# Hybrid encoder block with product-key experts: half of the far block's expert choice and 18 of its gathered products are made in the query stage

## Chip, cores, metric

The kernel runs on one core of a Trainium2 chip. The metric is the device time in microseconds of one execution, from three runs; a profile of one more execution is what the rows below come from. The engines are named as in the profile: PE (TensorE, its weight loads PEld), DVE (VectorE), ACT (ScalarE), POOL (GpSimd), SP (SyncE, which issues most transfers).

## The reference

One encoder block on 512 tokens of width 1024, in float32: a mixer (input projection, two recurrences, a short convolution, output projection, layer norm), then a layer of product-key experts and a last layer norm. The change is in the expert layer:

```python
q = (xt @ w_q).reshape(t, 8, 2, 128)                 # 8 heads, two halves
s1, s2 = q[:, :, 0] @ k1.T, q[:, :, 1] @ k2.T         # 128 keys each
v1, i1 = top_k(s1, 16);  v2, i2 = top_k(s2, 16)
cand_s = v1[..., :, None] + v2[..., None, :]          # 16 x 16 candidates
top_s, pos = top_k(cand_s, 16)
idx = take(i1 * 128 + i2, pos);  g = softmax(top_s)   # 16 of 16384 experts per head
act = gelu(einsum("cd,ced->ce", xb, u_tab[idx]))
y = einsum("ce,ced->cd", g * act, v_tab[idx])
```

So each token has 128 of 16384 experts, each one row of 1024 in a table u and one in a table v.

## The kernel before

The 512 tokens are four blocks of 128. For three of them (DTOK = 384 tokens) the layer is computed densely: for each of 128 blocks of 128 experts, `gelu(u block x tokens)` is multiplied by a gate matrix, which is zero where an expert was not chosen, and then by the v block. For the last, the "far" block (DT = 3), the chosen rows are gathered from HBM: 128 gathers of u rows (each [128 tokens x 1024], 0.5 MB) with one product and sum on DVE each, a gelu, then 128 gathers of v rows with a multiply-add each.

Each dense u block m goes through the same steps. SP loads `u_raw` (four buffers). PE transposes it in two halves (`turn`), ACT copies each half to `ut_hi` (`upper`), `ut_lo` is the difference (`lower`), PE makes 24 matmuls (`product`), ACT makes the gelu into `gel` (two buffers) and SP stores it to HBM (`activations`). ACT's gelu waits until the store that used its buffer has landed.

The program has four stages, and each engine runs its own list of instructions in order:

- The mixer, to about 341 us.
- The query stage: 16 steps n, one for each head and half, and three more u blocks. PE: query matmuls n, `turn(n + 1)`, `product(n)`, scores n. DVE: the 16 best of 128 scores for four token blocks; in odd steps also the 256 candidates and their 16 best. POOL: `lower(n - 1)`, then the lower half of the weight block, `wq_lo(n)`. Here the lower half of a u block is POOL's, and `turn(n + 1)` and `product(n)` wait for `lower(n)`.
- The gates stage: 77 steps s (u blocks 19 to 95). In blocks of four steps DVE turns the positions of one token block into expert numbers and gates (selection: `places`, `match`, `choose`, softmax); first the far block at s = 0, then block ST = 2, whose gates POOL scatters into the gate matrix in HBM one column at a time, then block 0. For blocks 0 and 1 a loop of 21 steps each (at s = 12 and 44) builds one-hot matrices whose products make the gates; each is stored in seven parts after its loop. I call the steps from one loop to the next the gap, and those behind the second loop the closing. `lower` is DVE's from here on. The far block's gathers are spread by `quarter_uses`; POOL starts gather q when product q - 4 is done (RING = 4 tiles).
- The experts stage: 128 steps n. Up to n = 64 (TAIL) every second step makes one of the last 32 u blocks, so a pair of steps is one product and two output steps; then only outputs. `used_by(n)` spreads what is left of the 256 gathered uses.

U_FROM = 72 is the number of gathered products made before the experts stage.

## Time and profile before

| | |
|---|---|
| median of 3 runs | 1733.19 us (1724.51 to 1734.79) |
| profiled execution | 1738.09 us |
| its span, first to last instruction | 1736.3 us |
| PE, DVE, ACT, POOL busy | 1648.8, 1250.3, 640.1, 822.1 us |
| DMA | 397.16 MB, mean 229 GB/s |

The profile's span lies inside the profiled execution's time; the 1.8 us between them are outside the program's instructions. Busy times of PE are modelled ends of pipelined matmuls, so a share near 95% says that PE has work, not that it is at its peak. "Idle before" is the time for which an engine sat idle, and the name behind the arrow is what ended it.

### The profile page before, as it was taken

Reading aid. Unit: us, or ns where it says so; the run is one execution under the profiler, and the core shown is the slowest. Engines: PE = TensorE matmul, PEld = TensorE weight load, DVE = VectorE, ACT = ScalarE, POOL = GpSimd, SP = SyncE. Lnnn points to the kernel's source line nnn. Section 1 sums busy time; section 2 is a strip of 40 time slices with the busy share of each in tenths; the row PEclk is TensorE's granted clock in tenths of the full one; section 3 lists DMA queues with packets and bytes.
Section 4 is the critical chain, followed back from the end, with each engine's and each line's share of the span. In section 5 each row is a group of like instructions: output and inputs, shape, how many; then the busy total and the mean of one; then the engine's idle time right before and its main releaser. Section 6 shows DMA issues by size and latency. Waiting matters only on the chain.

```text
span 1736.3 us, 23321 instructions
## 1 busy us (share of the span) xinstructions
PE 1648.8 (95%) x8522; PEld 1428.2 (82%) x8522; DVE 1250.3 (72%) x2436; ACT 640.1 (37%) x1053; POOL 822.1 (47%) x542
## 2 busy tenths in 40 slices
PE   7998989699999999999998889999999999999996
PEld 5876644499999999999998878888888887888885
DVE  6667842368888887856776368877777787788756
ACT  3568740323334333333333233333333333333331
POOL 4744520284433478877778234545565563222001
PEclk9999999899999999999999989999999999999998
DMA  8436200433324677799777999998999989999772
GB/s 269 145 103 200 85 0 0 136 116 98 106 79 149 177 189 215 212 316 268 208 203 213 364 372 349 332 347 315 326 321 346 324 311 344 341 355 359 234 233 88
DMA packets 242897, 397.16 MB, mean 229 GB/s; under 512 B 33704, under 2 KB 173408, under 8 KB 242784
## 3 DMA queue, kind: packets, MB, share of 16 engines
q1 hardware_dynamic: 182816, 259.17, 44.1%
q0 software_dynamic: 55296, 134.31, 25.0%
q10 hardware_dynamic: 4672, 2.19, 0.4%
q8 instruction: 68, 1.11, 0.3%
q14 instruction: 45, 0.37, 0.1%
HBM read 349.40 MB, written 46.20 MB: 228 GB/s over the span
## 4 chain that ended last, share of the span: by engine, by line
PE 43%; DMA 10%; DVE 8%; POOL 4%; issue 3%; ACT 1%; SPq 0%; POOLq 0%; DVEq 0%; ACTq 0%
PE bank L1544 24%; PE bank L841 13%; DMA activations<-gel 4%; DMA gathered<-in_peer_v,expert_rows 4%; PE bank L829 3%; POOL gate_matrix L209 3%; PE bank L1422 2%; DVE ut_lo L899 1%; POOL gathered L930 1%; DMA gathered<-in_peer_u,expert_rows 1%; DVE sel L1301 1%; DVE v_lo L1624 1%; DVE gather_sum L946 1%; DMA gate_rows_then_feed<-activations 1%; DVE hit L1291 1%
## 5 line engine op out<-in xcount | busy, mean ns | idle before, releaser
L841 PE MATMUL bank<-xhi,ut_hi 128*128 128x384 f32 x1024 | 355.1, 347 | 0.3 <-ACT gel L867 0.3
L841 PE MATMUL bank<-xhi,ut_lo 128*128 128x384 f32 x1024 | 344.7, 337 | 0.0
L841 PE MATMUL bank<-xlo,ut_hi 128*128 128x384 f32 x1024 | 344.3, 336 | 0.0
L930 POOL DMA_INDIRECT gathered<-in_peer_v,expert_rows x128 | 193.6, 1512 | 233.1 <-DVE gather_sum L946 216.1
L209 POOL DMA_INDIRECT gate_matrix<-gate_values,gate_cells x128 | 225.8, 1764 | 72.6 <-issue 36.9
L1544 PE MATMUL bank<-v_hi,w_hi 128*128 128x512 f32 x768 | 242.3, 397 | 11.0 <-DVE w_lo L1641 11.0
L930 POOL DMA_INDIRECT gathered<-in_peer_u,expert_rows x128 | 162.8, 1272 | 173.5 <-DVE gather_product L942 129.8
L1544 PE MATMUL bank<-v_lo,w_hi 128*128 128x512 f32 x768 | 238.8, 392 | 0.0
L1544 PE MATMUL bank<-v_hi,w_lo 128*128 128x512 f32 x768 | 238.7, 392 | 0.0
L899 DVE TENSOR_TENSOR ut_lo<-bank,ut_hi 128x512 fp32r<-128x512 f32 x216 | 141.8, 685 | 110.4 <-ACT ut_hi L858 104.6
L1578 ACT ACTIVATE v_hi<-gate_rows_then_feed 128x1024 fp32r<-128x1024 f32 x128 | 135.7, 1061 | 218.9 <-PE bank L1544 211.9
L1624 DVE TENSOR_TENSOR v_lo<-gate_rows_then_feed,v_hi 128x1024 fp32r<-128x1024 f32 x128 | 156.4, 1222 | 63.8 <-ACT v_hi L1578 63.1
L841 PEld LDWEIGHTS bank<-xhi,ut_hi 128*128 128x128 f32 x1024 | 194.3, 190 | 0.5 <-issue 0.5
L841 PEld LDWEIGHTS bank<-xlo,ut_hi 128*128 128x128 f32 x1024 | 194.2, 190 | 0.0
L841 PEld LDWEIGHTS bank<-xhi,ut_lo 128*128 128x128 f32 x1024 | 193.4, 189 | 0.0
L942 DVE SCALAR_TENSOR_TENSOR gather_product<-gathered,h 128x1024 f32<-128x1024 f32 x128 | 156.1, 1219 | 41.9 <-DMA gathered<-in_peer_u,expert_rows 38.4
L1544 PEld LDWEIGHTS bank<-v_hi,w_hi 128*128 128x128 f32 x768 | 142.7, 190 | 41.8 <-DVE v_lo L1624 12.1
L946 DVE SCALAR_TENSOR_TENSOR gather_sum<-gathered,expert_gates,gather_sum 128x1024 f32<-128x1024 f32 x128 | 160.7, 1279 | 21.6 <-DMA gathered<-in_peer_v,expert_rows 21.6
L1544 PEld LDWEIGHTS bank<-v_lo,w_hi 128*128 128x128 f32 x768 | 145.6, 190 | 30.8
L1544 PEld LDWEIGHTS bank<-v_hi,w_lo 128*128 128x128 f32 x768 | 145.3, 189 | 31.0
L858 ACT ACTIVATE ut_hi<-bank 128x512 fp32r<-128x512 f32 x256 | 145.4, 604 | 61.5 <-PE bank L829 60.8
L829 PE MATMUL bank<-ident,u_raw 128*128 128x128 f32 x1024 | 142.9, 278 | 23.7 <-DVE ut_lo L899 16.7
(183 smaller groups left out, 2499.4 us busy)
## 6 DMA issues: line engine op xcount, KB each, us to landing
u_raw<-in_peer_u SPq DMA_DIRECT2D x128, 512.0 KB
gate_rows_then_feed<-in_peer_v SPq DMA_DIRECT2D x128, 512.0 KB
gate_rows_then_feed<-gate_matrix SPq DMA_DIRECT2D x128, 192.0 KB
activations<-gel SPq DMA_DIRECT2D x96, 192.0 KB
gate_rows_then_feed<-activations SPq DMA_DIRECT2D x96, 192.0 KB
w_in<-in_w_in SPq DMA_DIRECT2D x28, 512.0 KB, 4.2
gate_matrix<-gate_zeros SPq DMA_DIRECT2D x8, 1024.0 KB, 6.9
wq<-in_peer_wq SPq DMA_DIRECT2D x16, 512.0 KB, 4.4
```

The costliest lines, as they stand in the source:

```text
L209: self.nc.gpsimd.indirect_dma_start(out=self.flat, out_offset=bass.IndirectOffsetOnAxis(ap=self.at[:, k:k + 1], axis=0), in_=self.gate[:, ...
L829: ins = self.nc.tensor.transpose(self.bank[b][:, k * P:(k + 1) * P], raw[:, j * P:(j + 1) * P], self.ident[:, :])
L841: ins = self.nc.tensor.matmul(self.bank[b + (r % 2) * spare][:, 0:DTOK], u[r % 2][:, k, :], x[:, k, 0:DTOK], start=(i == 0), stop=(i == 3 ...
L858: ins = self.nc.scalar.activation(self.hi[r % 2][at], turned, ACT.Copy)
L899: self.nc.vector.tensor_tensor(out=self.lo[r % 2][at], in0=self.bank[b].rearrange("p (k e) -> p k e", k=4), in1=self.hi[r % 2][at].bitcast ...
L930: self.nc.gpsimd.indirect_dma_start(out=self.tile[r][:, :], out_offset=None, in_=self.tables[kind], in_offset=bass.IndirectOffsetOnAxis(ap ...
L942: ins = V.scalar_tensor_tensor(out=self.product[:, :], in0=self.tile[r][:, :], scalar=1.0, in1=self.x, op0=ALU.mult, op1=ALU.mult, accum_o ...
L946: ins = V.scalar_tensor_tensor(out=y, in0=self.tile[r][:, :], scalar=self.gate[:, k:k + 1], in1=y, op0=ALU.mult, op1=ALU.add)
L1422: ins = nc.tensor.matmul(bank[4 + u][:, q * KEYS:(q + 1) * KEYS], second[:, u, q, :], first[:, u, q, :], start=True, stop=True)
L1544: ins = mm(bank[2 + 2 * tb + half][:, :], w[r][:, tb * P:(tb + 1) * P], v[r][:, half * HALF_D:(half + 1) * HALF_D], start=begins, stop=ends)
L1578: S.activation(v_hi[r][:, :], v_raw[r][:, :], ACT.Copy).then_inc(v_hi_ready, 1)
L1624: V.tensor_tensor(out=v_lo[r][:, :], in0=v_raw[r][:, :], in1=v_hi[r][:, :].bitcast(F32), op=ALU.subtract).then_inc(v_lo_ready, 1)
```

## The change

Heads 0 to 3 of the far block are chosen in the query stage: DVE does places, match and choose behind its step 7, the second match and choose behind step 8, softmax and the row list behind step 9; ACT makes the exponent in its step 8. POOL starts four gathers in its iteration 10, and then three in each iteration from 12 on; DVE makes three products at the head of each of its steps 11 to 15 and three behind them, 18 in all. In the gates stage the far block's selection has heads 4 to 7 alone, in three steps, and what follows comes one step earlier; outside of the loops half a gathered product is made a step where it was one. 80 products are made before the experts stage where it was 72; there two a step are used up to n = 64, where it was 2.25, so that 48 are left for the steps behind it (it was 40). The dense gelu has four buffers.

```diff
@@ -55,15 +55,19 @@
 
 MADE = 96
 RING = 4
-U_FROM = 72
+U_FROM = 80
+EARLY_HEADS = 4
+EARLY_USES = (0,) * 11 + (3,) * 5 + (3,)
+U_QUERIES = sum(EARLY_USES)
+GELS = 4
 ST = DT - 1
 NT, PARTS = 4, 7
 GROUPS = P // NT
 LOOP_STEPS = 21
-SELECT_AT = {DT: 0, ST: 4, 0: 8, 1: 33}
-LOOP_AT = (12, 44)
+SELECT_AT = {DT: 0, ST: 3, 0: 7, 1: 32}
+LOOP_AT = (11, 43)
 CLOSING_AT = LOOP_AT[1] + LOOP_STEPS
-SCATTER_AT = 8
+SCATTER_AT = 7
...
-        self.gel = sb("gel", [P, 2, DTOK])
+        self.gel = sb("gel", [P, GELS, DTOK])
         self.loaded = [sem(f"u_loaded{i}") for i in range(self.UB)]
         self.turned, self.hi_ready, self.lo_ready = sem("u_transposed"), sem("ut_hi_ready"), sem("ut_lo_ready")
         self.done, self.ready = sem("act_done"), sem("gelu_ready")
-        self.stored = [sem(f"act_stored{i}") for i in range(2)]
+        self.stored = [sem(f"act_stored{i}") for i in range(GELS)]
...
-        eng.dma_start(act_dram[at, :], self.gel[:, r % 2, :]).then_inc(self.stored[r % 2], 16)
+        eng.dma_start(act_dram[at, :], self.gel[:, r % GELS, :]).then_inc(self.stored[r % GELS], 16)
...
-        after(eng, self.stored[r % 2], 16 * stores)
+        after(eng, self.stored[r % GELS], 16 * stores)
...
+class Selection:
...
+    def places(self, link, tb, q, n):
+
+        V, heads = self.nc.vector, slice(q, q + n)
+        V.tensor_tensor(out=self.ex[:, 0:n, :], in0=self.top[:, tb, heads, :],
+                        in1=self.top[:, tb, heads, 0:1].broadcast_to([P, n, TOPK]),
+                        op=ALU.subtract).then_inc(self.less_max, 1)
+        V.tensor_scalar(out=self.place[:, 0, 0:n, :], in0=self.pos[:, tb, heads, :], scalar1=4, scalar2=None,
+                        op0=ALU.logical_shift_right)
+        V.tensor_scalar(out=self.place[:, 1, 0:n, :], in0=self.pos[:, tb, heads, :], scalar1=TOPK - 1, scalar2=None,
+                        op0=ALU.bitwise_and)
+        link(V.tensor_copy(self.keyf[:, 0:n, :, :], self.key[:, tb, heads, :, :]))
+        link(V.tensor_copy(self.placef[:, :, 0:n * TOPK], self.place[:, :, 0:n, :].rearrange("p s q k -> p s (q k)")))
+
+    def match(self, link, side, n):
+
+        V, shape = self.nc.vector, [P, n * TOPK, TOPK]
+        link(V.tensor_tensor(out=self.hit[:, 0:n, :, :].rearrange("p q k j -> p (q k) j"),
+                             in0=self.placef[:, side, 0:n * TOPK].unsqueeze(2).broadcast_to(shape),
+                             in1=self.iotab[:, :].unsqueeze(1).broadcast_to(shape), op=ALU.is_equal))
+
+    def choose(self, link, side, n):
+
+        V, hit = self.nc.vector, self.hit[:, 0:n, :, :]
+        link(V.tensor_tensor(out=hit, in0=hit, in1=self.keyf[:, 0:n, side, :].unsqueeze(2).broadcast_to([P, n, TOPK, TOPK]),
+                             op=ALU.mult))
+        link(V.tensor_reduce(self.sel[:, side, 0:n * TOPK], hit.rearrange("p q k j -> p (q k) j"), AX.X, ALU.add))
...
+    def list_rows(self, link, far, q, n):
+
+        link(self.nc.vector.scalar_tensor_tensor(
+            out=far.rows[:, q * TOPK:(q + n) * TOPK], in0=self.sel[:, 0, 0:n * TOPK], scalar=float(KEYS),
+            in1=self.sel[:, 1, 0:n * TOPK], op0=ALU.mult, op1=ALU.add))
+        self.nc.vector.sem_inc(far.listed, 1)
+
+
+    def exponent(self, eng, count, n):
+        eng.wait_ge(self.less_max, count)
+        self.nc.scalar.activation(self.ex[:, 0:n, :], self.ex[:, 0:n, :], ACT.Exp).then_inc(self.exp_ready, 1)
...
-        if q == 0:
-            eng.wait_ge(self.listed, 1)
+        if q in (0, EARLY_HEADS * TOPK):
+            eng.wait_ge(self.listed, 1 + q // (EARLY_HEADS * TOPK))
...
+        picks = Selection(nc, sem, sb, "early", EARLY_HEADS, iota, top, pos, key)
+        PICK_AT = 2 * EARLY_HEADS - 1
+        used_by = lambda n: sum(EARLY_USES[:n])
+        assert PICK_AT + 4 <= EARLY_USES.index(3) and len(EARLY_USES) == QC + 1
...
-                    acts.gelu_to_store(eng, n, n, n // 2)
+                    if n == PICK_AT + 1:
+                        picks.exponent(eng, 1, EARLY_HEADS)
+                    acts.gelu_to_store(eng, n, n, n // GELS)
...
+                    for q in range(RING) if n == PICK_AT + 3 else range(used_by(n - 1) + RING, used_by(n) + RING):
+                        far.start(eng, q)
                 for m in range(QC - 1, BY_QUERIES + 1):
                     acts.lower(eng, m, m)
+                    if m == QC - 1:
+                        for q in range(used_by(QC - 1) + RING, used_by(QC) + RING):
+                            far.start(eng, q)
...
+                picks.constants(link)
...
+                    for e in range(used_by(n), used_by(n + 1)):
+                        far.use(eng, e)
...
+                    if n == PICK_AT:
+                        picks.places(link, DT, 0, EARLY_HEADS)
+                        picks.match(link, 0, EARLY_HEADS)
+                        picks.choose(link, 0, EARLY_HEADS)
+                    elif n == PICK_AT + 1:
+                        picks.match(link, 1, EARLY_HEADS)
+                        picks.choose(link, 1, EARLY_HEADS)
+                    elif n == PICK_AT + 2:
+                        link(picks.softmax(eng, link, 1, EARLY_HEADS, far.gate[:, 0:EARLY_HEADS * TOPK]))
+                        picks.list_rows(link, far, 0, EARLY_HEADS)
+                for e in range(used_by(QC), used_by(QC + 1)):
+                    far.use(eng, e)
...
-            if at <= s < at + 4:
+            if at <= s < at + (3 if tb == DT else 4):
...
-            return int(SELECT_AT[0] <= s < LOOP_AT[0])
-        return 4
+            return int(SELECT_AT[ST] <= s < LOOP_AT[0])
+        return 2
...
-    used_by = lambda s: min(U_FROM, sum(quarter_uses(e) for e in range(s)) // 4)
+    used_by = lambda s: min(U_FROM, U_QUERIES + sum(quarter_uses(e) for e in range(s)) // 4)
+    started_by = lambda s: min(U_FROM, used_by(s) + RING) if s else U_QUERIES - EARLY_USES[QC] + RING
...
+            def select_far(part):
+
+                q, n = heads_of(DT)
+                if part == 0:
+                    picks.places(link, DT, q, n)
+                    picks.match(link, 0, n)
+                    picks.choose(link, 0, n)
+                elif part == 1:
+                    picks.match(link, 1, n)
+                    picks.choose(link, 1, n)
+                elif part == 2:
+                    link(picks.softmax(eng, link, nth[DT] + 1, n, far.gate[:, q * TOPK:(q + n) * TOPK]))
+                    picks.list_rows(link, far, q, n)
...
-                for q in range(used_by(s) + RING, min(used_by(s + 1) + RING, U_FROM)) if s else range(RING):
+                for q in range(started_by(s), started_by(s + 1)):
...
-    used_by = lambda n: min(2 * SLOTS, U_FROM + 9 * min(n, TAIL) // 4 + max(n - TAIL, 0))
+    used_by = lambda n: min(2 * SLOTS, U_FROM + 2 * min(n, TAIL) + max(n - TAIL, 0))
...
-                if n < 4:
-                    eng.wait_ge(acts.stored[m % 2], 16 * (MADE // 2))
+                if n < 2 * GELS:
+                    eng.wait_ge(acts.stored[m % GELS], 16 * (MADE // GELS))
                 else:
-                    eng.wait_ge(w_made, n - 3)
+                    eng.wait_ge(w_made, n - 2 * GELS + 1)
```

In the closing the number of uses goes from 12 to 4, in the seven steps of the gap behind the selection from 6 to 3; the rate in the loops stays at 1.25 a step, and so does that of the scatters.

## Rows read from the trace of the kernel before

**Rows 1.** The page: chain that ended last, by engine.

```profile
PE 43%; DMA 10%; DVE 8%; POOL 4%; issue 3%; ACT 1%; SPq 0%; POOLq 0%; DVEq 0%; ACTq 0%
```

**Rows 2.** Windows by stage: length, busy time of engines, granted clock, DMA share, GB/s.

```profile
341.50:537.80 196.30, 194.54 (x1096) 178.47 (x1096) 153.83 (x776) 70.87 (x128) 105.58 (x63) 0.99 0.32 102
...
603.20:737.90 134.70, 134.70 (x932) 134.70 (x931) 112.62 (x260) 49.74 (x128) 104.53 (x70) 1.00 0.76 207
737.90:799.70 61.80, 57.72 (x356) 56.44 (x354) 32.91 (x45) 19.87 (x38) 47.97 (x30) 0.97 1.08 325
799.70:941.40 141.70, 137.75 (x933) 136.54 (x931) 108.53 (x252) 49.93 (x128) 111.93 (x73) 0.99 0.76 201
941.40:1015.60 74.20, 64.55 (x383) 62.48 (x381) 30.32 (x50) 18.11 (x37) 26.95 (x22) 0.95 1.05 360
...
1041.10:1186.60 145.50, 145.50 (x750) 128.85 (x749) 119.75 (x188) 51.33 (x78) 71.30 (x50) 1.00 0.95 344
1186.60:1447.90 261.30, 254.01 (x1289) 223.01 (x1288) 208.42 (x238) 87.23 (x132) 150.58 (x87) 0.99 0.91 322
...
1470.90:1710.70 239.80, 238.49 (x1044) 196.95 (x1044) 177.36 (x223) 85.73 (x118) 33.39 (x33) 0.99 0.84 290
```

**Rows 3.** Timeline, ACT, two steps without gate work: start, duration.

```profile
532.73 0.49 ACT L867 ACTIVATE gel<-bank 128x384 f32<-128x384 f32 x1 [2.54 <-PE bank L841]
...
537.80 0.49 ACT L867 ACTIVATE gel<-bank 128x384 f32<-128x384 f32 x1 [2.56 <-PE bank L841]
```

**Rows 4.** Waits in the closing: engine, line, waited for: total us, times, longest.

```profile
ACT gel L867 <- DMA activations<-gel: 32.3, 6, 9.2
...
PEld bank L829 <- DMA u_raw<-in_peer_u: 8.8, 4, 3.0
```

**Rows 5.** POOL groups by form: count, busy us, mean ns, idle before.

```profile
L209 POOL DMA_INDIRECT gate_matrix<-gate_values,gate_cells x128 | 225.8, 1764 | 72.6 <-issue 36.9 <-DMA gate_matrix<-gate_values,gate_cells 20.5 <-DVEq L1319 15.2
L930 POOL DMA_INDIRECT gathered<-in_peer_v,expert_rows x128 | 193.6, 1512 | 233.1 <-DVE gather_sum L946 216.1 <-issue 15.3 <-DVE gather_product L942 1.7
L930 POOL DMA_INDIRECT gathered<-in_peer_u,expert_rows x128 | 162.8, 1272 | 173.5 <-DVE gather_product L942 129.8 <-issue 25.6 <-DVEq L1323 18.0
```

**Rows 6.** Timeline, POOL, beside the selection.

```profile
590.47 3.67 POOL L209 DMA_INDIRECT gate_matrix<-gate_values,gate_cells  x1 [0.30 <-issue]
```

**Rows 7.** Chain (first row) and DVE timeline, a 3-use step of the experts.

```profile
1192.84 10.58 DMA gathered<-in_peer_v,expert_rows
...
1203.45 1.28 DVE L946 SCALAR_TENSOR_TENSOR gather_sum<-gathered,expert_gates,gather_sum 128x1024 f32<-128x1024 f32 x1 [3.92 <-DMA gathered<-in_peer_v,expert_rows]
```

**Rows 8.** Timeline, DVE, steps 11 and 12 of the query stage.

```profile
476.87 0.89 DVE L1179 MAX8 best<-bank 128x8 f32<-128x128 f32 x4 [3.22 <-PE bank L1142]
...
491.28 0.89 DVE L1179 MAX8 best<-bank 128x8 f32<-128x128 f32 x4
...
499.73 0.89 DVE L1179 MAX8 best<-bank 128x8 f32<-128x128 f32 x4 [3.22 <-PE bank L1142]
```

**Rows 9.** Timeline, DVE, a selection; then the page's row of gathered products.

```profile
540.42 2.29 DVE L1291 TENSOR_TENSOR hit<-placef,iotab 128x2048 bf16<-128x2048 bf16 x1
...
543.95 1.22 DVE L1296 TENSOR_TENSOR hit<-hit,keyf 128x2048 bf16<-128x2048 bf16 x1
...
L942 DVE SCALAR_TENSOR_TENSOR gather_product<-gathered,h 128x1024 f32<-128x1024 f32 x128 | 156.1, 1219 | 41.9 <-DMA gathered<-in_peer_u,expert_rows 38.4
```

**Rows 10.** Timeline, POOL, query stage.

```profile
462.10 2.55 POOL L881 TENSOR_TENSOR ut_lo<-gather_sum,ut_hi 128x512 fp32r<-128x512 f32 x2 [6.57 <-ACT gather_sum L861]
464.60 2.41 POOL L1116 TENSOR_TENSOR wq_lo<-wq,wq_hi 128x1024 fp32r<-128x1024 f32 x1
```

**Rows 11.** Timeline, PE, query stage.

```profile
452.92 1.05 PE L1142 MATMUL bank<-keysT,qT 128*128 128x128 f32 x8
...
459.30 1.04 PE L829 MATMUL bank<-ident,u_raw 128*128 128x128 f32 x8
```

**Rows 12.** Windows at the end of the gap (columns as rows 2).

```profile
790.00:795.00 5.00, 2.51 (x11) 2.54 (x12) 3.12 (x5) 3.09 (x6) 4.08 (x4) 0.68 1.10 394
```

More of the change, by code:

```diff
@@ L1303, in softmax @@
[L1303 to L1313 removed]
+            picks.constants(link)
```

124 lines of the change are left out of this document (55 added, 69 removed).

## Prediction

> **What bounds the kernel now.** I read the chain of waits first: PE alone carries 43% of the span, with DMA 10% and DVE 8% behind [rows 1]. So a change pays only where PE waits, and it costs wherever it makes PE wait. The windows by stage show where that is [rows 2]. In the query stage (341.5 to 537.8) PE is busy 194.54 of 196.3 us: nothing can be won there, and PE itself sets the step. In the first loop of the gates stage (603.2 to 737.9) it is busy throughout. The gap between the loops (737.9 to 799.7, DMA share 1.08), the second loop (141.7 us for the same 21 steps) and the closing (941.4 to 1015.6, DMA share 1.05 at 360 GB/s) are where PE loses time. In the experts stage the window 1041.1 to 1186.6 holds 11 pairs of steps, 13.23 us each, PE busy throughout; 1186.6 to 1447.9 holds 19 pairs in 261.3 us, 9.9 us above 19 x 13.23. From 1470.9 on PE is busy 238.49 of 239.8 us. The eight gathers that the change adds there lie beside it, as DVE has 177.36 us of work in the same window; I put them at nothing.
>
> **Time that the change wins.** (1) Closing. A step without gate work takes 5.05 us, gelu to gelu [rows 3]; 12 of them make 60.6, the window has 74.2, so 13.6 us is the most that can be won. The waits there are gelu for its store (32.3 us in 6) and PE for u_raw (8.8 in 4) [rows 4]. The change uses 4 gathered rows in the closing where there were 12: eight times 0.524 MB (128 rows of 4 KB) is 4.2 MB, at 360 GB/s 11.7 us. Four gelu buffers let a store land nearly four steps late instead of two. I take 12, bounds 5 and 13.6. (2) Gap. 61.8 us less 11 x 5.05 and 1.8 or so for a group of gate matmuls leaves 4.4, with DMA as full as in the closing. Three or four gathers fewer and the spare gelu buffers should take nearly all: 4, bounds 1 and 4.4. (3) Second loop. It is 7.0 us longer than the first. POOL has 2.4 scatters of 1.764 us and 1.25 gathers of 1.272 us a step, each with 0.30 us of issue [rows 5, 6]: 4.95 + 1.97 = 6.9 us against a step of 134.7 / 21 = 6.4. It enters the loop late, since in the gap it has two scatters and one gather, 5.7 us, in 5.05; with half a gather it has 4.9. Over seven steps that is 5 us less delay: I take 5 of the 7.0, bounds 0 and 7. (4) Experts. In a 3-use step DVE waits 3.92 us for a gather that was 10.58 us on its way [rows 7]. At two uses a step each of the four tiles has a whole pair of steps, 13.2 us, for a start (1.512 + 0.30, [rows 5, 6]) and those 10.6. It just fits, with less traffic around it. Of 9.9 I take 9, bounds 5 and 9.9. Together 30, bounds 11 and 35.
>
> The half selection that is left in the gates stage I put at nothing: DVE's saved 6 us lie beside PE, whose steps there run at 5.05 or 0.2 above.
>
> **Time that the change costs: the query stage.** Two steps take 22.86 us. DVE's odd step takes 14.4 (476.87 to 491.28), the even one 5.2, and then DVE idles 3.22 [rows 8]. Added: a match over 2048 elements takes 2.29 us, the product of the two 1.22 [rows 9], and the reduce as long as the match. Half of each is about 1.2, 0.65 and 1.2; with 0.9 for the places, step 7 gets 3.9 us and step 8 gets 3.0; softmax and list put 0.9 into step 9. Eighteen products of 1.22 [rows 9] are 22 us. In all DVE gets 30 us.
>
> The order on POOL is what hurts. POOL runs ahead of DVE: its iteration n makes the lower half of u block n-1, then that of weight block n. In the trace the pair at 462.10 and the wq_lo at 464.60 are iteration 12 [rows 10], while DVE is in step 9. The change makes iteration 10 start the first gathers right behind its wq_lo, at 467.0 - 22.86 = 444.2. The first start waits until the rows are listed, which DVE does at the end of its step 9. That step's scores are made from 452.92 on [rows 11] and before the change DVE took them up at 476.87 - 22.86 = 454.0. Now it is 3.7 us late (3.9 + 3.0 added, 3.22 idle) and takes 14.4 + 0.9: it lists at 473.0. POOL then makes four starts, 1.57 each with issue (479.3), and only after them, in iteration 11, the lower half of u block 10, 2.5 more (481.8). What is queued behind this wait is thus the work that PE needs at 459.30, when the query matmuls end [rows 11]: the transposes of block 11 take over its bank, and product 10 reads it. PE goes on some **22 us** late (bounds 18 and 26).
>
> The same knot is tied again. POOL's iteration n also waits for three products at the head of DVE's step n-1. Where that stands behind an odd step (iterations 13 and 15), counted from the scores of the odd step: DVE is free at 14.65, its first product ends at 15.9, three starts one behind the other end at 20.6, the lower half at 23.1. PE wants it at 17.4 (11.42 + 5.6 + 0.4): 5.7 us each, **11.4** (bounds 0 and 16). The tail (three starts, then three products behind step 15) adds **3**. ACT's Exp in step 8 waits for DVE and puts two table loads before a gelu; PE needs that gelu's bank two steps later, so 0, at most 2. Last, after 2.6 us of idle PE the granted clock was 0.68 over 790 to 795 [rows 12], 1.6 us of full-clock work lost. Four stalls: **5** (0 to 7). The query stage costs 22 + 11.4 + 3 + 5 = 41, bounds 30 and 50.
>
> **Sum.** The profiled execution took 1738.1 us (span 1736.3): 1738.1 + 41 - 30 = 1749. It stands 4.9 above the median of the runs, 1733.2, so for the median I forecast 1733.2 + 11 = **1744 us**.
>
> **Rivals.** *A, POOL's wait is mostly hidden.* If POOL came to its wait only when the list is nearly there, what is left is DVE's overflow: 30 us of work in 13 us of idle time (four times 3.22), 17 at the end of the stage. 1733 + 17 - 30 = 1720. For it: DVE idles in every pair of steps. Against it: the program's order, by which PE can't reach the scores that end the wait's chain any sooner. 0.1. *B, the wait moves (slower).* The closing stays bound by DMA. With gelu's wait gone, gate stores of 1.18 MB, u blocks of 0.52 and gelus of 0.20 are still 1.90 MB a step, 5.3 us at 360 GB/s before any gather, and PE waits for u_raw instead. It decides if a u block lands more than three steps after its issue. Then closing and gap win 6 instead of 16 and the second loop nothing: 41 - 15 = 26, 1759. 0.22. *C, starts get longer beside DVE.* One scatter next to DVE's selection took 3.67 us [rows 6] against a mean of 1.764. If a third of the query stage's starts took 2 us more, each knot would hold 1 to 3 us more, some 8 in all: 1752. 0.1.
>
> The Trainium skill (SBUF — State Buffer, section SBUF: two separate sides) says that VectorE's two-port operations and GpSimd share one pair of ports as an exclusive lock, and that the descriptors of a gather wait for it; by that rule C holds. The one long scatter agrees, the mean shows that most starts are not held.
>
> *The forecast* itself has 0.58, and 1733 to 1756 as its own range.
>
> **How the numbers follow.** About 1% (17 us) tells a change of this kernel from none: 1716 and 1750.5. Slower by more: B 0.2, C 0.07, and 0.1 of the forecast's upper end, 0.37. Faster by more: a third of A and the ends of the gains, 0.06. Between: 0.57. The range 1722 to 1762 takes in B, C and the near edge of A.
>
> **What would show it.** Right: in the query stage one PE gap of about 22 us near 460, ended by POOL's ut_lo, two of 5 to 6, and a stage of about 237 us; POOL's first gather waiting some 29 us for DVE; closing steps of 5.1 to 5.4 us with no wait of gelu for its store; 19 pairs of the experts at 13.2 to 13.4. Wrong: a stage only 17 us longer (A), waits for u_raw over 15 us in the closing (B), starts above 2 us in the query stage (C).

## The result and the profile after

The changed kernel takes 1743.81 us (median of 7 runs, 1741.59 to 1747.21), the kernel before 1733.19 in the 7 runs beside them (1724.16 to 1737.39). The ratio is 1.0076, 95% interval 1.0049 to 1.0103: slower by 0.8%, less than the 1% that I took as the bound. The profiled execution took 1745.51 us, its span 1743.7.

First the chain of waits of the kernel after, by engine.

```profile
PE 60%; DVE 3%; DMA 2%; issue 1%; ACT 1%; SPq 0%; POOL 0%; POOLq 0%; DVEq 0%; ACTq 0%
```

Against [rows 1] DMA has gone from 10% to 2% and DVE from 8% to 3%. Nothing of that tells that the kernel got slower. For this the windows by stage are needed, with the columns of [rows 2]: length, busy PE, PEld, DVE, ACT, POOL, granted clock, DMA share, GB/s.

```profile
338.00:574.00 236.00, 200.08 (x1105) 181.41 (x1103) 186.53 (x824) 76.30 (x134) 129.84 (x82) 0.93 0.39 127
574.00:643.70 69.70, 65.90 (x402) 64.81 (x403) 59.40 (x91) 27.64 (x48) 23.73 (x17) 0.95 0.55 163
643.70:778.20 134.50, 134.50 (x928) 134.47 (x926) 110.54 (x250) 52.12 (x129) 105.46 (x70) 1.00 0.78 207
778.20:838.50 60.30, 56.85 (x362) 55.57 (x360) 30.27 (x46) 17.74 (x37) 46.80 (x31) 1.00 1.09 316
838.50:971.60 133.10, 133.10 (x918) 133.07 (x916) 106.86 (x246) 49.25 (x126) 104.88 (x70) 1.00 0.78 207
971.60:1039.10 67.50, 63.09 (x387) 61.45 (x386) 20.01 (x32) 18.56 (x36) 11.49 (x10) 0.97 1.05 344
1064.50:1210.10 145.60, 145.60 (x751) 128.96 (x750) 115.07 (x175) 51.21 (x78) 67.64 (x45) 1.00 0.90 314
1210.10:1461.10 251.00, 251.00 (x1290) 222.30 (x1289) 195.35 (x227) 87.84 (x132) 141.46 (x78) 1.00 0.92 319
1478.00:1718.00 240.00, 240.00 (x1060) 198.46 (x1058) 188.01 (x233) 87.10 (x119) 42.38 (x42) 1.00 0.89 313
```

Line by line against [rows 2]: the query stage 236.0 (196.3 before), the gap 60.3 (61.8), the second loop 133.1 (141.7), the closing 67.5 (74.2), the 19 pairs of the experts 251.0 (261.3), with PE busy throughout. The windows of gap and second loop are cut one step off the loop, which now comes a step earlier; by the same blocks the second loop is 134.7 against 141.6 (table below). 251.0 / 19 is 13.21 us a pair, which is the 13.23 of the undisturbed pairs. So each of the four places named in the prediction got shorter, and the query stage paid for more than all of them.

Where it paid, PE's timeline shows. The first row is PE's last matmul before it stops, the others are the four that it starts late on.

```profile
456.00 0.39 PE L1241 MATMUL bank<-xhi,wq_lo 128*128 128x512 f32 x1
477.05 2.25 PE L833 MATMUL bank<-ident,u_raw 128*128 128x128 f32 x8 [20.67 <-POOL ut_lo L885]
...
518.33 2.25 PE L833 MATMUL bank<-ident,u_raw 128*128 128x128 f32 x8 [4.93 <-POOL ut_lo L885]
...
548.85 2.25 PE L833 MATMUL bank<-ident,u_raw 128*128 128x128 f32 x8 [5.78 <-POOL ut_lo L885]
...
557.81 0.63 PE L833 MATMUL bank<-ident,u_raw 128*128 128x128 f32 x4 [1.00 <-POOL ut_lo L885]
```

Each time PE waits for `ut_lo`, POOL's lower half. POOL's own timeline says what it was doing instead.

```profile
438.66 2.42 POOL L1198 TENSOR_TENSOR wq_lo<-wq,wq_hi 128x1024 fp32r<-128x1024 f32 x1
470.67 1.20 POOL L1005 DMA_INDIRECT gathered<-in_peer_u,expert_rows  x1 [29.59 <-DVEq L970]
472.17 0.95 POOL L1005 DMA_INDIRECT gathered<-in_peer_u,expert_rows  x1 [0.30 <-issue]
473.43 0.94 POOL L1005 DMA_INDIRECT gathered<-in_peer_u,expert_rows  x1 [0.30 <-issue]
474.68 0.93 POOL L1005 DMA_INDIRECT gathered<-in_peer_u,expert_rows  x1 [0.30 <-issue]
475.63 2.50 POOL L885 TENSOR_TENSOR ut_lo<-gather_sum,ut_hi 128x512 fp32r<-128x512 f32 x2
```

POOL stood 29.59 us at the first gather, until DVE had listed the rows (released from line 970). Then it made four starts in 4.9 us, and only then the lower half for which PE waited.

The reader should also see what this does to DVE, whose load matters below: after the list it has nothing to do, since PE is late with the scores.

```profile
470.08 0.22 DVE L967 SCALAR_TENSOR_TENSOR expert_rows<-sel_early 128x64 int32<-128x64 f32 x1
485.09 0.89 DVE L1267 MAX8 best<-bank 128x8 f32<-128x128 f32 x4 [14.78 <-PE bank L1229]
```

Before, that idle time was 3.22 us [rows 8].

Last the waits in the closing of the kernel after.

```profile
PEld bank L833 <- DMA u_raw<-in_peer_u: 5.8, 5, 2.4
ACT ut_hi L862 <- PE bank L833: 4.9, 3, 2.3
PE bank L833 <- DMA u_raw<-in_peer_u: 4.4, 3, 2.1
```

The 32.3 us of gelu's wait for its store [rows 4] are gone from the list; the waits for `u_raw` are not.

### A table of stages

For all kernels of this study I took the starts of ACT's gelu instructions from the timeline; the dense u blocks are numbered by them, so that the lengths can be compared. "Query" is from the gelu of block 0 to that of block 20; "gates" all from there to block 95 (selection, first loop, gap, second loop, closing); "pairs" the 19 pairs of the experts; "rest" what follows to the end. One profiled execution each.

| kernel | query | first loop | gap | second loop | closing | gates | pairs | rest |
|---|---|---|---|---|---|---|---|---|
| before | 199.3 | 134.7 | 61.9 | 141.6 | 74.2 (12 steps) | 466.0 | 261.3 | 288.3 |
| after | 243.1 | 134.7 | 59.9 | 134.7 | 72.1 (13 steps) | 448.8 | 251.0 | 282.6 |

In the difference of the spans, 7.4 us, stand +43.8 (query), -17.2 (gates), -10.3 (pairs), -5.7 (rest), and -3.1 in the mixer, which the change doesn't touch. The gelu of block 0 starts at 350.2 us in this execution of the kernel before and between 346.3 and 348.2 in the twelve others, so these 3.1 us look like chance in one execution.

### The profile page after: what moved, and what is told of

Same layout as the page of the kernel before. It is cut to its first block, busy times and chain, and to the rows that moved or that the text cites. A ratio compares the mean times of both kernels' runs of the same rounds, so it can differ in the third digit from the quotient of the medians.

```text
span 1743.7 us, 23338 instructions
## 1 busy us (share of the span) xinstructions
PE 1644.4 (94%) x8522; PEld 1427.4 (82%) x8522; DVE 1259.2 (72%) x2452; ACT 644.1 (37%) x1056; POOL 820.4 (47%) x542
## 3 DMA queue, kind: packets, MB, share of 16 engines
q10 hardware_dynamic: 4672, 2.19, 0.4%
## 4 chain that ended last, share of the span: by engine, by line
PE 60%; DVE 3%; DMA 2%; issue 1%; ACT 1%; SPq 0%; POOL 0%; POOLq 0%; DVEq 0%; ACTq 0%
PE bank L1619 29%; PE bank L845 22%; PE bank L833 5%; PE bank L1497 3%; DMA u_raw<-in_peer_u 2%; DVE sel_late L954 1%; DVE ut_lo L903 1%; DVE hit_late L952 0%; DVE hit_late L945 0%; SPq L817 0%; ACT L975 0%; ACT v_hi L1653 0%; POOL rs L1692 0%; DVE bn L1753 0%; DVE h L1795 0%
## 5 line engine op out<-in xcount | busy, mean ns | idle before, releaser
L1005 POOL DMA_INDIRECT gathered<-in_peer_u,expert_rows x128 | 161.0, 1257 | 257.2 <-DVE gather_product L1017 201.1
L213 POOL DMA_INDIRECT gate_matrix<-gate_values,gate_cells x128 | 222.1, 1735 | 56.8 <-issue 36.9
L833 PEld LDWEIGHTS bank<-ident,u_raw 128*128 128x128 f32 x1024 | 121.6, 143 | 66.0 <-issue 42.1
```

The lines of the kernel that those rows point to most:

```text
L213: self.nc.gpsimd.indirect_dma_start(out=self.flat, out_offset=bass.IndirectOffsetOnAxis(ap=self.at[:, k:k + 1], axis=0), in_=self.gate[:, ...
L833: ins = self.nc.tensor.transpose(self.bank[b][:, k * P:(k + 1) * P], raw[:, j * P:(j + 1) * P], self.ident[:, :])
L1005: self.nc.gpsimd.indirect_dma_start(out=self.tile[r][:, :], out_offset=None, in_=self.tables[kind], in_offset=bass.IndirectOffsetOnAxis(ap ...
```

## Experiments

Each ratio is against runs of the kernel before on the same chip. The first four ran together, so did the next four, and the last three; the kernel before had medians of 1732.53, 1732.29 and 1728.96 us beside them, so kernels of different groups are compared by their ratios or by their stages.

### 1. POOL's gathers two iterations later

```diff
-   for q in range(RING) if n == PICK_AT + 3 else range(used_by(n - 1) + RING, used_by(n) + RING):
+   for q in (range(RING) if n == PICK_AT + 5 else range(used_by(n - 2) + RING, used_by(n - 1) + RING)
+             if n > PICK_AT + 5 else ()):
        far.start(eng, q)
...
-   if m == QC - 1:
-       for q in range(used_by(QC - 1) + RING, used_by(QC) + RING):
+   if m in (QC - 1, QC):
+       for q in range(used_by(m - 1) + RING, used_by(m) + RING):
```

> Kernel after, with POOL starting the same 18 + 4 gathers two iterations later in the query stage; DVE's program is unchanged. Theory (POOL's order is what costs): DVE's list comes 8.7 us after POOL reaches the place instead of 29.6, the lower halves of the u blocks are no longer behind a wait that matters, and what is left is DVE's overflow (30 us of work in some 14 of idle time). Query stage of 236 us becomes some 213 to 216, no PE gap above 3 us in it; total 1743.8 - 20 to 23, 1721 to 1724. Rival (DVE's added work is the cost, POOL's wait only shows it): the stage stays near 236 and the time at 1744. Rival (the starts are slow beside DVE): gathers come late, the stage gets to 225, 1733.

Measured: 1730.73 us, ratio 0.9984 (0.9967 to 1.0001). The query stage is 228.7 us, 14.4 less than after and still 29.4 more than before. POOL's wait for the list and PE's timeline:

```profile
471.02 1.20 POOL L1005 DMA_INDIRECT gathered<-in_peer_u,expert_rows  x1 [6.97 <-DVEq L970]
```

```profile
508.03 2.25 PE L833 MATMUL bank<-ident,u_raw 128*128 128x128 f32 x8 [6.78 <-POOL ut_lo L885]
...
536.92 2.25 PE L833 MATMUL bank<-ident,u_raw 128*128 128x128 f32 x8 [8.68 <-POOL ut_lo L885]
...
545.88 0.63 PE L833 MATMUL bank<-ident,u_raw 128*128 128x128 f32 x4 [1.81 <-POOL ut_lo L885]
```

The list wait shrank from 29.59 to 6.97 us and PE's stop at 456 is gone, as expected. But the later stops grew from 4.93 and 5.78 to 6.78 and 8.68. The theory's number (1721 to 1724) was missed by 7 and its stage (213 to 216) by 13: something that the first stop had covered came up. Two things could be it. One is seen in a row, a product that took 6.04 us instead of 1.22, beside two instructions of POOL:

```profile
475.95 6.04 DVE L1017 SCALAR_TENSOR_TENSOR gather_product<-gathered,h 128x1024 f32<-128x1024 f32 x1
...
476.00 2.55 POOL L885 TENSOR_TENSOR ut_lo<-gather_sum,ut_hi 128x512 fp32r<-128x512 f32 x2
...
478.50 2.40 POOL L1198 TENSOR_TENSOR wq_lo<-wq,wq_hi 128x1024 fp32r<-128x1024 f32 x1
```

The other is DVE's load as such. DVE's timeline parts them. From the head of its step 7, at 427.2 us, to its last product, which ends at 561.4, it has no idle time: 134.2 us, where the kernel before has 105.8 for the same steps, 28.4 less. In experiment 9, with the same products and no gathers, 24.8 of these 28.4 are there. So DVE's load sets the length of this stage. PE's stops for `ut_lo` add nothing of their own, since DVE never ran dry behind them, and some 3.6 us are what DVE and POOL do to each other.

### 2. The kernel after with two gelu buffers

```diff
-GELS = 4
+GELS = 2
```

> Kernel after, with two gelu buffers again. Theory (the buffers carry what was won in gap and closing): gelu waits for its store again, some 15 to 30 us in the gap and closing together, and the time is 5 to 9 us more, 1749 to 1753. Rival (the eight gathers fewer are what won it, the buffers follow): gelu's waits stay under 8 us and the time is within 2 us of 1744.

Measured: 1742.24 us, ratio 1.0065 (1.0042 to 1.0087), beside 1.0076 for the kernel after. The waits in its closing:

```profile
ACT gel L871 <- DMA activations<-gel: 30.0, 7, 5.6
...
PEld bank L833 <- DMA u_raw<-in_peer_u: 5.3, 4, 2.0
```

Gelu waits 30 us for its stores again and the closing is 70.6 us for 13 steps, not longer than the 72.1 with four buffers. So that wait costs nothing, and in this kernel the buffers bring nothing.

### 3. The kernel before with four gelu buffers

```diff
+GELS = 4
...
-        self.gel = sb("gel", [P, 2, DTOK])
+        self.gel = sb("gel", [P, GELS, DTOK])
```

(and every `% 2` and `// 2` of the gelus as in the change)

> Kernel before, with four gelu buffers and nothing else. Theory (half of the closing's loss is gelu waiting for its store): the closing of 74.2 us gets to 68 to 70, the gap wins 1 to 3, second loop and experts stay: 1733.2 - 6 to 9, 1724 to 1727. Rival (the closing is bound by DMA, 26.7 MB at 360 GB/s): PE waits for u_raw instead, the closing stays above 73 us, 1731 to 1734.

Measured: 1730.39 us, ratio 0.998 (0.9955 to 1.0005): no difference that can be told. In its closing (73.3 us, before 74.2) PE waits for `u_raw` instead:

```profile
PEld bank L830 <- DMA u_raw<-in_peer_u: 12.2, 6, 3.7
...
PE bank L830 <- DMA u_raw<-in_peer_u: 10.3, 5, 3.4
```

That was 8.8 us in 4 for PEld before [rows 4]. The wait moved, and the closing stayed bound by DMA. The profiled execution here was one of the short ones, 1721.89 us, 8.5 below the median, so the shorter second loop and pairs that the table below has for it are no gain of the median.

### 4. The kernel before with two gathered uses a step

```diff
-    used_by = lambda n: min(2 * SLOTS, U_FROM + 9 * min(n, TAIL) // 4 + max(n - TAIL, 0))
+    used_by = lambda n: min(2 * SLOTS, U_FROM + 2 * min(n, TAIL) + 17 * max(n - TAIL, 0) // 16)
```

> Kernel before, with 2 instead of 2.25 gathered uses a step up to step 64 of the experts stage and 17 in 16 steps behind it; nothing in the query and gates stages. Theory (the ring of four tiles can't turn 3 uses in a step): the 19 pairs of 261.3 us get to 251.4 and the 6 us at the handover to the pure output steps go too: 1733.2 - 16, 1717. Rival (the traffic is only moved, and the output steps at a DMA share of 0.96 to 0.99 give it back): the output steps of 239.8 us get 5 to 15 us longer, 1722 to 1732. Rival (in the changed kernel it was the smaller total of gathers left, 176 against 184, that helped): less than 8 us won, 1725 or more.

Measured: 1718.84 us, ratio 0.9917 (0.9891 to 0.9942). The 19 pairs take 251.0 us (261.3 before) and the rest 284.3 (288.3). So this one line, which needs no product in the query stage, brings what the change brought in the experts stage, all 10.3 us of the pairs and 4.0 of the rest.

### 5. Both of these edits

The kernel before with the edits of experiments 3 and 4.

> Kernel before with two gathered uses a step up to n = 64 of the experts stage and four gelu buffers. The two edits gave 13.7 us and 2 us (not told from none) each by itself. Theory: they add nothing to one another; four buffers are worth nothing where the closing is bound by DMA, so this is 1717 to 1719 (ratio to before 0.991 to 0.993), query stage 199.3, V window 251.0. Rival: the buffers remove gelu's waits for its store in the closing and give 4 us or more on top, 1713 or less.

Measured: 1717.02 us, ratio 0.9905 (0.9871 to 0.9938). Stages: gates 462.7, pairs 251.0, rest 283.8. It is the base for the next kernels, which have four gelu buffers and two uses a step too.

### 6. The early selection alone

From the kernel after: no gather and no product in the query stage.

```diff
-U_FROM = 80
+U_FROM = 72
-EARLY_USES = (0,) * 11 + (3,) * 5 + (3,)
+EARLY_USES = (0,) * 17
...
-   for q in range(RING) if n == PICK_AT + 3 else range(used_by(n - 1) + RING, used_by(n) + RING):
-       far.start(eng, q)
...
-   started_by = lambda s: min(U_FROM, used_by(s) + RING) if s else U_QUERIES - EARLY_USES[QC] + RING
+   started_by = lambda s: min(U_FROM, used_by(s) + RING) if s else 0
```

(outside of the loops one product a step again; the experts' `used_by` as in experiment 4)

> Kernel after with the early choice of four heads alone in the query stage: no gathers and no products there (72 products in the gates stage as before, two uses a step in the experts up to n = 64, then 17/16). Theory: the selection's 8 us on DVE (3.9 in step 7, 3.0 in step 8, 0.9 in step 9) lie in idle times of 3.22 us each and beside PE, so the query stage is 199.3 plus 0 to 2 and the kernel stands 0 to 2 us from the same kernel without it, 1717 to 1721. Rival: the selection itself already delays DVE so that s_used or the banks stop PE; then a good part of the 43.8 us shows here, 1725 or more.

Measured: 1713.2 us, ratio 0.9884 (0.9851 to 0.9917). The query stage takes 199.4 us: choosing the first four heads there costs nothing. Against experiment 5, run beside it, it is 3.8 us less; the intervals of the two ratios overlap. But it takes up DVE's reserve: from the head of step 7 to the end of the stage's work DVE had 12.9 us of idle time before, and here it has 1.3.

### 7. The early selection and the first four starts

```diff
+   for q in range(RING) if n == PICK_AT + 3 else ():
+       far.start(eng, q)
```

> The last kernel plus the first four starts of gathers in POOL's iteration 10 of the query stage, as in the kernel after; no product there (its first is in the gates stage). So this is the first knot alone. Theory: POOL waits some 29 us for the row list, PE idles 20 to 21 us for ut_lo near 456, 2 to 3 us more go to the clock behind it; the query stage is 220 to 224, the kernel 21 to 24 us above the early selection alone, some 1740 to 1743. Rival: PE's delay is partly given back (no backlog on DVE as there are no products), 10 us or less above it; or the knot costs more than its stall (clock), 28 or more.

Measured: 1736.27 us, ratio 1.0016 (0.9995 to 1.0037), 23.1 us above the kernel of experiment 6. The query stage takes 222.0 us, 22.6 more. PE's row:

```profile
476.85 2.25 PE L833 MATMUL bank<-ident,u_raw 128*128 128x128 f32 x8 [20.66 <-POOL ut_lo L885]
```

That is the stop of the kernel after (20.67 us) to 0.01 us, with four starts and no product anywhere in the stage. Of the 1.9 us beside it nearly all is PE at the lower of its clock levels after the stop: the granted clock was 0.50 until 480.3 us, 3.5 us of work. This is the first knot of the prediction, alone.

### 8. Fewer gathers in the gap and the closing, nothing in the query stage

From experiment 5:

```diff
-U_FROM = 72
+U_FROM = 63
...
-        return 4
+        return 2
...
-17 * max(n - TAIL, 0) // 16
+5 * max(n - TAIL, 0) // 4
```

> The first kernel of this batch with 63 products before the experts stage instead of 72: half a gathered product a step in the gap and the closing as in the kernel after, nothing in the query stage, and 5/4 uses a step from n = 64 of the experts on (65 there, it was 56). So it takes the gathers out of the gap and the closing without the query stage's cost. Theory: what the kernel after gained there (gap 2, selection, second loop and closing together 17.2 with one step less of selection) comes from DMA's load, so closing and gap are 6 to 9 us shorter, the nine more uses lie beside PE (DVE has 50 us free there), 1709 to 1713. Rival: the closing is bound by u blocks, gate stores and gelus alone and the gap as well, 2 us or less gained, or the last 64 steps take back what is won: 1717 or more.

Measured: 1706.8 us, ratio 0.9847 (0.9816 to 0.9878), 10.2 us below experiment 5 and more than the 4 to 8 that I had expected. The closing, 12 steps in either, in windows (first experiment 5, then this one):

```profile
936.50:1009.80 73.30, 64.63 (x382) 62.44 (x381) 30.50 (x50) 18.80 (x37) 26.42 (x22) 0.95 1.07 369
```

```profile
931.10:997.10 66.00, 61.09 (x382) 59.55 (x381) 22.31 (x36) 18.60 (x38) 15.58 (x14) 1.00 1.06 355
```

The closing is 7.3 us shorter and moves 23.4 MB instead of 27.0 (length times rate), so 3.6 MB less; at 369 GB/s that would have been 9.8 us, but the rate fell to 355. DMA's share stays at 1.06, and PE still waits for `u_raw`, 4.8 us in 3: it is still bound by DMA. The nine products moved to the end cost 2.4 us there (rest 286.2 against 283.8).

### 9. Eighteen products, but no gathers

Experiment 6 with the products of the kernel after on data that is in SBUF anyway.

```diff
+   for e in range(3) if n >= 11 else ():
+       link(V.scalar_tensor_tensor(out=far.product[:, :], in0=h[:, 0, :], scalar=1.0, in1=far.x,
+                                   op0=ALU.mult, op1=ALU.mult, accum_out=far.act[:, e:e + 1]))
```

(and three more behind step 15)

> The kernel with the early selection alone (1713.2 us, query stage 199.4) plus 18 products on DVE, three at the head of each of steps 11 to 15 and three behind step 15, as in the kernel after; but they multiply two blocks of h in SBUF instead of a gathered tile, their sums go to the columns of the activations that are written again later, and POOL starts no gather in the query stage. So DVE has the work and POOL and DVE can hold each other up, but POOL waits for nothing of DVE. Theory: of the 21 us between the first four starts alone (query stage 222.0) and the kernel after (243.1), most is POOL waiting for products in front of its lower half; DVE's work alone adds 6 to 10 us (22 us of products against 3.22 us of idle time in each pair of steps), query stage 205 to 210, kernel 1719 to 1724. Rival 1: DVE's load is the cost by itself, whatever POOL waits for: 15 us or more. Rival 2: hardly any (under 3 us), all of it was POOL's order.

Measured: 1739.08 us, ratio 1.0053 (1.0028 to 1.0078). The query stage takes 225.3 us, 25.9 more than without the products. I had expected 6 to 10; the first rival held. In windows, the last 24 us of it by themselves:

```profile
431.00:535.00 104.00, 103.69 (x594) 95.17 (x592) 101.51 (x399) 39.94 (x71) 45.49 (x28) 1.00 0.29 96
535.00:559.00 24.00, 0.01 (x1) 0.04 (x1) 22.95 (x88) 0.49 (x1) 0.14 (x1) 0.56 0.02 8
```

PE runs to 535 without a stop, and then stands for 24 us, in which DVE is the only engine at work. The start of the gates stage is a point where all engines meet, and DVE comes to it last:

```profile
558.99 1.30 PE L833 MATMUL bank<-ident,u_raw 128*128 128x128 f32 x5 [24.02 <-PEq L1135]
```

DVE has 101.51 us of work in the 104 before 535 and waits for nobody in them: its backlog can't get smaller there. How large it is, DVE's rows at the two ends show, first of the kernel before, then of this one:

```profile
431.15 0.89 DVE L1179 MAX8 best<-bank 128x8 f32<-128x128 f32 x4 [3.21 <-PE bank L1142]
...
539.09 0.17 DVE L1273 CAST iotab<-iota 128x16 bf16<-128x16 f32 x1 [2.12 <-PEq L1056]
```

```profile
427.72 0.89 DVE L1261 MAX8 best<-bank 128x8 f32<-128x128 f32 x4 [3.22 <-PE bank L1223]
...
558.84 0.18 DVE L926 CAST iotab_late<-iota 128x16 bf16<-128x16 f32 x1 [0.54 <-PEq L1135]
```

The first row of each is the head of step 7, the second the first work behind the meeting point. Before, DVE was done at 536.97, 105.8 us after the head of step 7, of which it idled 12.9 (four times 3.2), and then it waited 2.12 us for the others. Here it is done at 558.30, 130.6 us after it, with no idle time. So the change's work on DVE is 37.6 us, and what doesn't fit into the idle time is 24.8. 18 products in this stage cost some 26 us even where POOL waits for nothing of DVE.

### 10. Six products instead of 18

From the kernel after: `EARLY_USES = (0,) * 11 + (1,) * 5 + (1,)`, POOL's starts as in experiment 1, `U_FROM = 70`, 5/4 uses a step from n = 64 on.

> One gathered product instead of three in each of DVE's steps 11 to 15 and behind them, 6 in all, with POOL's first four starts in its iteration 12, where the rows are listed, and the later ones two iterations behind those of the kernel after; half a product a step in the gap and the closing as in the kernel after; 70 before the experts stage, 5/4 uses a step from n = 64 on. Theory: DVE has idle time for one product a step (3.22 us in a pair, 2.44 us of products), and POOL's list wait of 7 us and its 1 us starts are the only cost: query stage plus 3 to 8 over 199.4, which eats what six gathers fewer at the end bring (0 to 2 us): 1707 to 1713. Rival: POOL's starts and lower halves lie beside DVE's work and hold one another up as with three products: plus 15 or more, 1718 or more. Rival: free, 1705 or less.

Measured: 1713.82 us, ratio 0.9915 (0.9885 to 0.9944). Query stage 209.0 us, 9.6 above the early selection alone; I had said 3 to 8. The reserve that I counted on, 3.22 us in two steps, had gone to the selection (1.3 us left in experiment 6), and the six products took 12.7 us on DVE, one of them 6.01 beside POOL. Here too DVE has no idle time up to the meeting point.

### 11. The early selection, and fewer gathers at the end of the gates stage

Experiment 6 with `U_FROM = 64`, half a product a step outside of the loops, and 5/4 uses a step from n = 64 on.

> The same without any gather or product in the query stage: early selection, half a product a step in the gap and the closing, 64 before the experts stage, 5/4 uses a step from n = 64 on. Theory: the gains of the early selection alone (about 4 us over the same kernel without it, one step more for the closing) and of fewer gathers at the end of the gates stage (10 us) add up only in part, because both act on the same closing bound by DMA: 1702 to 1706. Rival: they add, 1701 or less; or the 4 us were chance, 1707.

Measured: 1704.67 us, ratio 0.9861 (0.9831 to 0.9891): the lowest median of all, 2.1 us below experiment 8, where the early selection is not made. But by the ratio experiment 8 is the lower one (0.9847), and each ratio lies inside the other's interval: the two can't be told apart, and the early selection is worth nothing that shows. Against experiment 10, which differs by the six products in the query stage, it is 9.2 us less, as much as the query stages differ (209.0 against 199.4). In the profiles the six gathers fewer later on show as 3.6 us in the rest (286.5 against 290.1) and 2.4 us the other way in the gates; in the medians they brought nothing.

| kernel | query | first loop | gap | second loop | closing | gates | pairs | rest | median us |
|---|---|---|---|---|---|---|---|---|---|
| 1 POOL two later | 228.7 | 134.7 | 59.5 | 136.3 | 75.9 (13) | 453.8 | 251.0 | 282.7 | 1730.73 |
| 2 after, two gelus | 242.6 | 134.7 | 60.6 | 134.7 | 70.6 (13) | 448.0 | 251.0 | 282.6 | 1742.24 |
| 3 before, four gelus | 199.3 | 134.7 | 61.1 | 134.7 | 73.3 (12) | 457.4 | 256.5 | 289.2 | 1730.39 |
| 4 before, two a step | 199.3 | 134.7 | 62.6 | 142.2 | 71.5 (12) | 464.6 | 251.0 | 284.3 | 1718.84 |
| 5 both | 199.4 | 134.7 | 61.6 | 139.5 | 73.3 (12) | 462.7 | 251.0 | 283.8 | 1717.02 |
| 6 early selection | 199.4 | 134.7 | 65.1 | 135.3 | 76.9 (13) | 459.4 | 251.0 | 284.4 | 1713.20 |
| 7 first four starts | 222.0 | 134.7 | 59.8 | 142.6 | 76.7 (13) | 461.2 | 251.0 | 283.8 | 1736.27 |
| 8 fewer at the end | 199.3 | 134.7 | 60.9 | 134.7 | 65.9 (12) | 449.8 | 251.1 | 286.2 | 1706.80 |
| 9 products, no gathers | 225.3 | 134.7 | 62.9 | 135.2 | 78.2 (13) | 458.4 | 251.0 | 283.9 | 1739.08 |
| 10 six products | 209.0 | 134.7 | 59.5 | 134.7 | 73.0 (13) | 449.7 | 251.1 | 286.5 | 1713.82 |
| 11 selection, fewer at end | 199.4 | 134.7 | 57.4 | 135.4 | 72.4 (13) | 447.3 | 251.0 | 290.1 | 1704.67 |

## Why the prediction was right, and where it wasn't

**The time.** 1744 was forecast for the median and 1743.81 measured; for the profiled execution 1749, and 1745.5 measured. Of the 3.5 us between them 3.1 are in the mixer. That the median fits to 0.2 us is luck: the seven runs of the kernel before spread over 13 us, and the profiled execution, on which the forecast was built, stood 4.9 us above the median before and 1.7 after. The forecast's own case is what happened, none of the rivals as a whole. But two errors of its terms offset one another, and one of its reasons doesn't hold.

**The first knot, 22 us: right.** 20.67 us of stop in the kernel after, 20.66 by itself (experiment 7), with POOL's wait at 29.59 where 29 was forecast. The term was 1.3 us too large because the four starts took 4.9 us and not 6.3: 0.94 each behind the first, where the mean of the row I took was 1.272 [rows 5].

**The later knots, 11.4, and the tail, 3: the size right, the reason only in part.** Measured 4.93 + 5.78 = 10.7, and 1.00 + 3.21 = 4.2 (the last is PE's stop at 573.9, where the engines meet before the gates stage; 1.5 of it stood there before the change, which leaves 2.7). I wrote that the order on POOL is what hurts. For the first knot experiment 7 shows it. For the rest it is not the cause: take the waits of POOL away and leave the products, and the stage is 25.9 us longer all the same (experiment 9), with the whole of it in one stop at the end. The step that failed is the one that priced these stops as waits of POOL for products. They are for the most part how DVE's load comes to the surface. In the kernel after DVE idles only 5.6 us between the first stop and the meeting point (2.40, 0.69 and 2.52, waiting for scores), and it is the last to arrive; so, by an estimate from these rows, POOL's waits can hold no more than that of the 21.1 us by which the stage is longer than in experiment 7. My rival A had this mechanism and gave it 17 us, for a kernel without POOL's waits; experiment 9 has 24.0 us of stop. The load was taken too low, 30 us where 37.6 were measured: the products take 26.1 us from start to start and not 22 (15 of them 1.449 us instead of 1.224, and each has the read of its sum behind it), the selection 10.6 and not 8, and the candidate sums 1.2 more; both of the last two are longer beside POOL. 37.6 less the 12.9 of idle time is 24.8, within rounding. In the kernel before DVE was done 0.7 us ahead of PE's last matmul, and PE itself ends 0.7 us later here, so DVE ends 23.3 us behind PE; 0.7 more pass until PE starts again, which makes the stop of 24.0.

The two causes are also not independent. The first knot costs 22.6 us alone, the load of DVE 25.9 alone, both together 43.8 and not 48.5; in the first stop DVE catches up and idles 14.78 us. And moving POOL's starts out of DVE's way (experiment 1) gave back 14.4 us, not 22.6. I should have worked out DVE's load as a bound of its own (backlog at the meeting point) and not only the chain over POOL.

**The clock, 5: too small.** The stops are 35.6 us, 1.5 of which the kernel before had too; 43.8 less 34.1 leaves 9.7. The granted clock was 0.50 for 3.6 us of PE's work behind the first stop, and for 3.3, 3.4 and 5.9 behind those at 518, 549 and 577, 16.2 us in all. Eight transposes took 2.25 us behind a stop and 1.04 at the full clock [rows 11]; if all of that work took half as long at the full clock, 8.1 us are the clock's by this estimate, and 1.6 stay open.

**Query stage, 41 in all:** 43.8, inside the bounds of 30 and 50.

**The starts on POOL.** Rival C came true in small: a start beside a product took 1.88 us instead of 0.95, one in each group of three (last section). The forecast's price of 1.57 for every start, with issue, covers it: a group of three took 4.4 us where 4.7 stood.

**The closing, 12: mis-sized.** It won 6.7 (67.5 against 74.2 for the same twelve blocks). That is 5.6 us a step, above the 5.1 to 5.4 that I had named as a sign. Experiment 8 shows the gathers' share alone, 7.3. I had 4.2 MB less to move; 3.5 were seen to go (length times rate), and the rate fell as well, from 360 to 344 GB/s. I had counted on the four gelu buffers too, and they are worth nothing (experiments 2 and 3): this is the part of rival B that came true, in experiment 3 the wait moved to `u_raw`. The rest of B did not: the waits for `u_raw` in the kernel after stayed below its sign of 15 us (5.8 for the weight loads, 4.4 for the matmuls), and the other gains stood. The half of the selection that went, which I had put at nothing, brought 1.6 us.

**The gap, 4: about 2.** 59.9 against 61.9. With the usual rate of gathers the later kernels had 59.8 to 65.1, with half of it 57.4 to 60.9.

**The second loop, 5: 7 in the profile, but it varies.** The six kernels with half a product a step outside of the loops have 134.7 four times, 135.4 and 136.3; the seven with a whole one, the kernel before among them, have 134.7, 135.2, 135.3, 139.5, 141.6, 142.2 and 142.6. The kernels of experiments 6 and 7 have the same gates stage, except for the four gathers started earlier, and differ by 7.3 us. So nearly the same program can lose these 7 us or not, and with fewer gathers ahead of the loop it lost at most 1.6. What tips it was not settled; the mechanism was argued from POOL's rows [rows 5] and not tested by itself.

**The experts, 9: 10.3.** And 5.7 us more in the handover and after it that I hadn't seen: experiment 4 gets 4.0 of them by its one line. In the kernel before PE is idle 2.4 of the 23.0 us behind the pairs, and DVE waits there for `activations`; I had left this out of the sum.

In all the gains were 33.2 us where 30 stood, the costs 43.8 where 41 stood.

**What the change was worth.** Its selection in the query stage costs nothing by itself (experiment 6) and brings nothing that can be told (experiments 8 and 11), its two uses a step bring 14 us without it (experiment 4), its thinner closing brings 7 to 10 without it (experiment 8), and its four gelu buffers nothing. The 18 gathered products in the query stage, with the starts on POOL that they need, pay for none of these: they are the whole cost. Without them, and with the products that are then missing at the end of the experts stage, the other edits give 1704.67 us, 1.4% below the kernel before (0.9861) and, by the two ratios to it, 0.9861 / 1.0076, 2.1% below the kernel after.

## What to carry to other kernels

Before work is moved into a stage that is full on one engine, add it up for each other engine against its idle time up to the next point where the engines meet; what exceeds it comes out at that point (24.8 us of it as a stop of 24.0 in experiment 9), even where no wait of another engine stands in between. An engine that runs ahead of the others (here POOL, by three steps) must not be given a wait for the engine that runs behind in front of work that a third one needs. And when a change has several parts, each can be worth its own run: here one line had most of the gain, and one part all of the cost.

## What the runs showed of the hardware

**DVE and POOL hold each other up in SBUF.** In experiment 9 there are no gathers in the stage, so the two products beside POOL's lower half can be read by themselves:

```profile
525.48 1.23 DVE L1277 SCALAR_TENSOR_TENSOR gather_product<-h 128x1024 f32<-128x1024 f32 x1
...
526.17 3.90 POOL L885 TENSOR_TENSOR ut_lo<-gather_sum,ut_hi 128x512 fp32r<-128x512 f32 x2 [2.51 <-ACT gather_sum L865]
...
526.75 2.19 DVE L1277 SCALAR_TENSOR_TENSOR gather_product<-h 128x1024 f32<-128x1024 f32 x1
...
528.99 2.18 DVE L1277 SCALAR_TENSOR_TENSOR gather_product<-h 128x1024 f32<-128x1024 f32 x1
```

Two halves of POOL took 3.90 us instead of 2.55, and two products 2.19 and 2.18 instead of 1.23. The groups of this engine show the mean of the 15 products in the steps, 1449 ns, and of the three behind them, where POOL was idle, 1224:

```profile
L1277 DVE SCALAR_TENSOR_TENSOR gather_product<-h 128x1024 f32<-128x1024 f32 x15 | 21.7, 1449 | 0.4
...
L1300 DVE SCALAR_TENSOR_TENSOR gather_product<-h 128x1024 f32<-128x1024 f32 x3 | 3.7, 1224 | 0.1
```

The Trainium skill (SBUF — State Buffer, section SBUF: two separate sides) says that an operation of VectorE with two inputs in SBUF and one of GpSimd that reads SBUF lock the shared ports for a whole instruction; these rows agree. The 6.04 us of experiment 1 show more: there the product ends 1.1 us after the second of two POOL instructions in a row, so it was not let in between them. A product of experiment 9, with no gather about, took 2.73 us beside one POOL instruction and ended 1.1 us after it too.

**A gather's start is held by a product too.** In the kernel after, the first of each group of three starts lies beside DVE's next product:

```profile
491.56 1.23 DVE L1017 SCALAR_TENSOR_TENSOR gather_product<-gathered,h 128x1024 f32<-128x1024 f32 x1
```

```profile
491.73 1.88 POOL L1005 DMA_INDIRECT gathered<-in_peer_u,expert_rows  x1 [6.47 <-DVE gather_product L1017]
...
495.24 0.94 POOL L1005 DMA_INDIRECT gathered<-in_peer_u,expert_rows  x1 [0.30 <-issue]
```

All five groups of the stage show it: 1.88 us for the first start, 1.02 for the second, 0.94 for the third. In experiment 10 DVE makes no further product beside the start, and there the five take 0.95 us each. So a group of three is 1.0 us longer by it. That is rival C's mechanism at the lower edge of the 1 to 3 us that it gave each knot; its sign, starts above 2 us, did not appear, and it stays small beside DVE's load. The rule quoted in the prediction is about two-port operations; the product here is one with two inputs in SBUF, so what holds the start here was seen and not explained.

**What one start costs POOL.** Undisturbed starts took 0.93 to 0.96 us, alone (experiment 10) or with 0.30 of issue right behind another, and the first on a new list 1.20; the mean of all 128 starts of u rows in the kernel after is 1257 ns.
